# Feed-forward products of a four-layer decoder step in half blocks by seven products, with weight sums on POOL

## The reference

```
def causal_conv(x, buf, w):
    K = w.shape[0]
    T = x.shape[1]
    xp = jnp.concatenate([buf.astype(x.dtype), x], axis=1)
    y = xp[:, 0:T] * w[0]
    for j in range(1, K):
        y = y + xp[:, j:j + T] * w[j]
    return y, xp[:, T:]

def conv_ffn(x, buf, p, l):
    u, buf_new = causal_conv(x @ p['ffn_w_up'][l], buf, p['ffn_conv_w'][l])
    u = u + p['ffn_conv_b'][l]
    return (jax.nn.silu(u[..., :D_FF]) * u[..., D_FF:]) @ p['ffn_w_down'][l], buf_new
```

## Time and profile before

| | us |
|---|---|
| median of three runs | 3059.74 |
| lowest, highest | 3055.54, 3061.55 |
| the profiled execution | 3057.75 |
| its span, first to last instruction | 3056.1 |
| PE busy in it | 2891.5 (95%) |
| DVE busy | 1504.9 (49%) |
| ACT busy | 849.6 (28%) |
| POOL busy | 442.3 (14%) |

### The profile page before, as it was taken

One profiled execution on the slowest core, in us unless ns is written; L12 is line 12 of the kernel. 1 busy time (PEld: TensorE's weight loads), 2 busy tenths in 40 slices (PEclk: granted clock), 3 DMA queues, 4 the chain that ended last, 5 costly groups with the idle time before them and its releaser, 6 DMA issues.

```text
span 3056.1 us, 53572 instructions
## 1 busy us (share of the span) xinstructions
PE 2891.5 (95%) x20903; PEld 2108.9 (69%) x20903; DVE 1504.9 (49%) x2809; ACT 849.6 (28%) x2445; POOL 442.3 (14%) x1043
## 2 busy tenths in 40 slices
PE   7999999999988889999999899999998999989998
PEld 4788667766765567766766787867764678757765
DVE  7454548712333327741642454238715864438741
ACT  2334321102522221111555443211102134332111
POOL 0022111101222111101100221011100003202100
PEclk9999999999999999999999996799999999999999
DMA  5420123345223323333433013433342330123332
GB/s 160 146 57 7 44 91 121 115 119 120 67 77 92 89 74 111 124 114 112 138 101 101 6 40 95 131 124 120 109 121 87 118 98 5 30 76 110 124 105 83
DMA packets 401942, 287.48 MB, mean 94 GB/s; under 512 B 74956, under 2 KB 398077, under 8 KB 401309
## 3 DMA queue, kind: packets, MB, share of 16 engines
q1 hardware_dynamic: 382768, 267.03, 29.0%
q10 hardware_dynamic: 14828, 14.93, 1.5%
q0 software_dynamic: 4096, 2.11, 0.3%
HBM read 263.29 MB, written 20.73 MB: 93 GB/s over the span
## 4 chain that ended last, share of the span: by engine, by line
PE 88%; DVE 6%; ACT 2%; issue 2%; SPq 1%; DMA 1%; POOL 1%; ACTq 0%; DVEq 0%; POOLq 0%
PE bank L349 85%; SPq L2647 1%; PE bank L2821 1%; POOL arena L1345 1%; DMA arena<-cache_mla_latent 1%; PE bank L2844 0%; DVE h L1684 0%; DVE post_scaled L462 0%; DVE x L465 0%; PE bank L1297 0%; DVE small L1116 0%; DVE arena L1232 0%; DVE arena L1234 0%; DVE h L444 0%; DVE h L1683 0%
## 5 line engine op out<-in xcount | busy, mean ns | idle before, releaser
L349 PE MATMUL bank<-h,weights 128*128 128x320 f32 x3728 | 1018.4, 436 | 17.8 <-ACT h L431 17.8
L349 PEld LDWEIGHTS bank<-h,weights 128*128 128x128 f32 x3728 | 710.1, 191 | 322.3 <-issue 33.7
L349 PE MATMUL bank<-arena,weights 128*128 128x320 f32 (+4 forms) x3152 | 844.4, 434 | 15.5 <-DVE arena L1234 7.1
L349 PEld LDWEIGHTS bank<-arena,weights 128*128 128x128 f32 (+2 forms) x3152 | 584.1, 189 | 272.3 <-issue 26.2
L349 PE MATMUL bank<-arena 64*64 64x64 f32 (+8 forms) x2802 | 331.1, 289 | 9.7 <-DVE arena L2446 5.1
L462 DVE SCALAR_TENSOR_TENSOR post_scaled<-h,params,rstd 128x320 f32<-128x320 f32 x64 | 42.1, 658 | 543.9 <-ACT rstd L425 543.9
L349 PEld LDWEIGHTS bank<-arena 64*64 64x64 f32 (+3 forms) x2802 | 248.8, 163 | 35.7 <-issue 11.4
L1345 POOL TENSOR_TENSOR arena<-arena,consts 128x256 f32<-128x256 f32 x162 | 118.5, 736 | 779.9 <-DVE arena L1672 462.0
L570 ACT ACTIVATE arena<-bank 128x256 f32<-128x256 f32 x160 | 61.3, 383 | 541.0 <-PE bank L349 531.8
L638 DVE RECIPROCAL arena<-arena 128x336 f32<-128x336 f32 x88 | 197.6, 2246 | 0.0
L416 ACT ACTIVATE squares<-bank 128x320 f32<-128x320 f32 x64 | 28.0, 437 | 518.8 <-PE bank L349 518.8
(11 more groups left out here) (334 smaller groups left out, 3216.9 us busy)
## 6 DMA issues: line engine op xcount, KB each, us to landing
weights<-ffn_w_up SPq DMA_DIRECT2D x88, 1024.0 KB, 5.1
weights<-ffn_w_down SPq DMA_DIRECT2D x64, 704.0 KB, 4.7
weights<-rw_wrkv SPq DMA_DIRECT2D x24, 1024.0 KB, 5.3
weights<-gdn_w_in SPq DMA_DIRECT2D x24, 1024.0 KB, 5.4
arena<-cache_mla_latent SPq DMA_DIRECT2D x128, 128.0 KB, 2.3
weights<-rw_wo SPq DMA_DIRECT2D x8, 1024.0 KB, 5.4
weights<-gdn_wo SPq DMA_DIRECT2D x8, 1024.0 KB, 5.7
arena<-state_gdn_S SPq DMA_DIRECT2D x30, 256.0 KB, 4.0
```

What stands on the lines that cost most here:

```text
L349: return pe.matmul(out, lhsT, rhs, start=first, stop=last, skip_group_check=True)
```

## The change

Slots 3 to 21 of the up part, and all of the down part, are computed by seven products of half blocks (the Winograd form of Strassen's scheme): the weights of a slot are split in four quarters (two halves of the rows by two tiles of output), the activations in four (two halves of the k tiles by columns 0 to 159 and 160 to 319).

- PE makes m1, m6, m5, m7, m2, m3, m4 in this order, each over half of the k tiles, with 160 columns. Four banks serve a slot: m2 adds to m1, m4 to m7.
- POOL forms four sums of weight quarters for each slot (pool_sums) into one of three buffers; it gives its copies to ACT.
- DVE forms four sums of activation quarters (dve_mixes), once for H and in pieces for HFF after chunks 2, 3, 6, 7, 9 and 10, and combines the products out of PSUM.
- ACT takes over tap 2, the state columns, the kept rows, and the whole sigmoid as exp, ln(1 + e), exp.
- Down weights are loaded in 4 x 3 slots of 8, 8 and 6 k tiles by 256 columns. The turning of the last rows comes after the first pair of down tiles.

The diff, cut to its core:

```diff
+        def pool_sums(pool, key):
+
+            (a11, a12, a21, a22), (s1, s2, s3, s4) = quarters(key)
+            pool.wait_ge(*at(f"slot{where[key] % NS}", key))
+            if sum_of[key] >= NSUM:
+                pool.wait_ge(*at(*weight_used[summed[sum_of[key] - NSUM]]))
+            pool.tensor_tensor(s1, a21, a22, ALU.add).then_inc(*to("s1", key))
+            pool.wait_ge(*at("s1", key))
+            pool.tensor_tensor(s2, s1, a11, ALU.add).then_inc(*to("s2", key))
+            pool.tensor_tensor(s3, a11, a21, ALU.add).then_inc(*to("s3", key))
+            pool.wait_ge(*at("s2", key))
+            pool.tensor_tensor(s4, s2, a12, ALU.add).then_inc(*to("s4", key))
+
+        def dve_mixes(dve, dst, b1, b2, key):
+
+            b11, b12, b21, b22 = b1[:, :, 0:HN], b1[:, :, HN:NT], b2[:, :, 0:HN], b2[:, :, HN:NT]
+            t1, t2, t3, t4 = dst
+            dve.tensor_tensor(t1, b12, b11, ALU.subtract).then_inc(*to("mix1", key))
+            dve.tensor_tensor(t3, b12, b22, ALU.subtract).then_inc(*to("mix3", key))
...
+        def pe_fast_up(pe, l, c, half):
...
+            made = {"m1": ("fa", ("c11", key)), "m6": ("fb", ("c12", key)), "m5": ("fc", ("tt", key)), "m7": ("fd", ("c21", key))}
+            for step in PRODUCTS:
+                if step in made:
+                    ps = bank(pe, (made[step][0], key), made[step][1])[:, 0:HN]
+                elif step == "m2":
+                    ps = of(("fa", key))[:, 0:HN]
+                    pe.wait_ge(*at("s1c", key))
+                elif step == "m3":
+                    ps = of(("fb", key))[:, HN:NT]
+                    pe.wait_ge(*at("u2", key))
+                else:
+                    ps = of(("fd", key))[:, 0:HN]
+                    pe.wait_ge(*at("c22", key))
...
+                for k in range(4):
+                    ins = mm(pe, ps, a[:, k, :], b(k), k == 0 and step not in ("m2", "m4"), k == 3)
+                ins.then_inc(*to(step, key))
+            weight_used[key] = ("m4", key)
...
+            def gate_sigmoids(c):
+
+                for m in (2 * c, 2 * c + 1):
...
+                    act.activation(e, CONV[:, 0, m % 2, :], ACT.Exp, scale=-1.0).then_inc(*to("gate_e", (l, m)))
+                    act.wait_ge(*at("gate_e", (l, m)))
+                    act.activation(e, e, ACT.Ln, bias=1.0).then_inc(*to("gate_ln", (l, m)))
+                    act.wait_ge(*at("gate_ln", (l, m)))
+                    act.activation(e, e, ACT.Exp, scale=-1.0).then_inc(*to("gate_s", (l, m)))
...
+            for s in range(len(UP) + 1):
+                if s >= 1:
+                    first_taps(s - 1)
+                if FAST <= s < len(UP):
...
+                    act.activation(S1C[s % 2], of(("fa", key))[:, 0:HN], ACT.Copy).then_inc(*to("s1c", key))
+                if s >= 1:
+                    tails(s - 1)
...
+                if FAST <= s < len(UP):
...
+                    act.wait_ge(*at("m2", key))
+                    act.activation(XP[:, 2 * s % 4, 2:2 + HN], of(("fa", key))[:, 0:HN], ACT.Copy).then_inc(*to("c11", key))
+                if s >= 2 and s % 2 == 0:
+                    gate_sigmoids(s // 2 - 1)
+                if 1 <= s < len(UP) - 1:
+                    states(s + 1)
...
         def pool_ffn(pool, l):
             pool.wait_ge(*at("rstd", 4 * l + 2))
...
+            for s in range(FAST, len(UP)):
+                pool_sums(pool, slot_key(l, s))
+            for c in range(4):
+                for part in range(3):
+                    pool_sums(pool, ("down", l, c, part))
...
         def dve_ffn(dve, l):
             q = 4 * l + 2
             dve_scale_h(dve, q, ("up_done", (l, 1, 1)))
...
+            dve_mixes(dve, [UMIX[:, i] for i in range(4)], H[:, 0:4, :], H[:, 4:8, :], ("up", l))
...
+            for s in range(1, len(UP) + 1):
+                key = slot_key(l, s) if FAST <= s < len(UP) else None
+                conv(2 * s - 2)
+                if key:
...
+                    dve.tensor_tensor(U2, fb[:, 0:HN], S1C[s % 2], ALU.subtract).then_inc(*to("u2", key))
+                conv(2 * s - 1)
+                if key:
...
+                    dve.tensor_tensor(TT, fc[:, 0:HN], U2, ALU.add).then_inc(*to("tt", key))
+                    dve.wait_ge(*at("m7", key))
+                    dve.wait_ge(*at("tt", key))
+                    last_half(2 * s + 1, "c22", key, fd, TT, ALU.add)
+                if s % 2 == 0:
+                    gate(s - 2)
+                    gate(s - 1)
+                if key:
+                    dve.wait_ge(*at("m3", key))
+                    last_half(2 * s, "c12", key, fb[:, HN:NT], TT, ALU.subtract)
+                    dve.wait_ge(*at("m4", key))
+                    dve.tensor_tensor(XP[:, (2 * s + 1) % 4, 2:2 + HN], fd[:, 0:HN], U2, ALU.add).then_inc(*to("c21", key))
+                if s % 2 == 0 and s // 2 - 1 in MIXED:
```

More of the change, by code:

```diff
@@ L152 @@
     "rwkv_chunk_sums": "am inv y state m0 z sam m_new",
-    "ffn_taps": "tap1 tap2 conv",
-    "ffn_gate": "gate_d gate_gu gate_r hff",
+    "ffn_taps": "tap1 conv xp_zero",
+    "ffn_gate": "gate_gu hff",
+    "fast_products": "m1 m2 m3 m4 m5 m6 m7 part_done",
+    "fast_weights": "s1 s2 s3 s4",
+    "fast_activations": "mix1 mix2 mix3 mix4",
+    "fast_tiles": "u2 tt vv c11d c12 c21 c22",
+    "fast_copies": "s1c c11",
+    "ffn_sigmoid": "gate_e gate_ln gate_s",
+    "ffn_rows": "xp_state tail tap2",
     "residual": "x post",
@@ new lines, in build, with tile_pairs, quarters @@
+        UP = [(c, half) for c in range(11) for half in range(2)]
+        FAST = 3
+        summed = [key for l in range(layers) for key in
+                  [("up", l, half, c) for c, half in UP[FAST:]] + [("down", l, c, part) for c in range(4) for part in range(3)]]
+        sum_of = {key: i for i, key in enumerate(summed)}
+        def tile_pairs(key):
+            return DOWN_ROWS[key[3]][1] // 2 if key[0] == "down" else 4
+        def quarters(key):
+            kp = tile_pairs(key)
+            w = slot_view(where[key], 2 * kp, 256)
+            sums = arena(SUM0 + sum_of[key] % NSUM * 2048, 4, kp, P)
+            return [w[:, 0:kp, 0:P], w[:, kp:2 * kp, 0:P], w[:, 0:kp, P:256], w[:, kp:2 * kp, P:256]], [sums[:, i] for i in range(4)]
@@ L515, in build, with slot_key, xp_ready @@
         order = list(ffn_tiles())
-        def xp_step(l, n):
+        def slot_key(l, s):
+            return ("up", l, UP[s][1], UP[s][0])
+        def xp_ready(l, n):
             c, half, j, m = order[n]
-            return ("xp_first" if n < 4 else "xp", (l, half, m))
+            if n < 4:
+                return [("xp_first", (l, half, m))]
+            if n // 2 < FAST:
+                return [("xp", (l, half, m))]
+            return [("c22", slot_key(l, n // 2)), ("c21", slot_key(l, n // 2))] if j else \
+                   [("c11", slot_key(l, n // 2)), ("c12", slot_key(l, n // 2))]
         def pe_ffn(pe, l):
@@ L528, in pe_ffn @@
                 weight_used[("up", l, half, 0)] = ("up_done", (l, half, 1))
-            for n, (c, half, j, m) in enumerate(order):
+            for n, (c, half, j, m) in enumerate(order[0:2 * FAST]):
                 if n < 4:
@@ L540, in pe_ffn, with pe_tails @@
                 weight_used[key] = ("up_done", (l, half, m))
+            for c, half in UP[FAST:]:
+                pe_fast_up(pe, l, c, half)
+            for c in range(4):
+                pe_fast_down(pe, l, c)
+                if c == 0:
+                    pe_tails(pe, l)
+            pe_norm(pe, q + 1)
+        def pe_tails(pe, l):
             for g, (first, n) in enumerate([(0, 4), (4, 3)]):
@@ L576, in act_ffn @@
                     if m >= 2:
[L577 to L588, removed]
-                act.dma_start(rows[i * P:i * P + r, :], TOUT[0:r, 1 + i, :]).then_inc(*to("tail_stored", l, 16))
-            act_outputs(act, q + 1, ("tail_stored", l))
+                        act.wait_ge(*at("hff", (l, m - 2)))
@@ L635, in gate @@
[L635 to L641 removed]
+                dve.tensor_tensor(GD[:, 0, :], g, u, ALU.mult).then_inc(*to("gate_gu", (l, m)))
@@ L667, in build @@
+            dve_post_norm(dve, q + 1, lambda m: ("c21" if m % 2 else "c12", ("down", l, m // 2)))
         stage_x = arena(0, 3, D)
```

245 lines of the change are left out of this document (192 added, 53 removed).

## The result

The median went from 3057.64 us (3050.67 to 3061.55, four runs) to **3129.55 us** (3119.59 to 3132.02, four runs): a ratio of 1.0232, 95% interval 1.0202 to 1.0262. Slower, as forecast, and 25 us above the number given. The profiled execution took 3130.85 us, its span is 3129.1 us. The matmul helper of the changed kernel is L357. What follows is its last layer's feed-forward part, which runs from 2804 to 3109 us. From the pre-norm's last matmuls to the post-norm's first, each of the four layers took 276.8 us before and takes 294.9, 296.1, 296.8 and 295.6 us now: 76 us in all, where the whole span grew by 73. Each of the waits that the change brings to PE agrees within 0.5 us in the four layers.

What follows compares the result with a forecast made beforehand. PE's matmuls were taken to bound the kernel. Per layer, -33.2 (PE) + 34.9 (pairs) + 8 (start's wait) + 1.7 (half clock) = +11.4 us, times 4 = +46, giving 3105 us; range 2955 to 3180.

Steps and rivals of the forecast that it cites:

- PE's own part: Feed-forward matmuls: 1680 products of 160 columns at 135 ns replace 960 of 320, gaining 33.2 us a layer if PE never waits.
- PE's gain is no gain: Rival named with the experiments: the block scheme itself is no gain; no chance given.
- POOL's part: Weight sums: four additions of 512 columns a slot, 1.265 us each, 5.06 us a slot, fitting alone under 7.56.
- The lock: DVE and POOL exclude each other on SBUF operands; a sum ahead of a DVE operation costs 1.0 us, a handover saving 0.25.
- rival C: DVE and POOL handovers save nothing: 18 us a layer more, 3177 us; chance 0.02.
- A plain pair: Two up slots without mixing, scheduled by hand: 17.7 us instead of 15.1.
- one sum in its way: Step in the pair of slots: the second gate's last product meets one POOL sum and ends at 10.5 us.
- A mixing pair: Two up slots with DVE's mixing of gate tiles ahead: 20.0 us, against 16.9 without any lock.
- Rival B: PE's waits of 1 to 3 us in each pair bring half-clock windows, 15 us a layer, 3166 us; chance 0.08.
- The start: Up part's first slots: PE waits 8 us before m3 of slot 3, and half clock costs 1.7 us.
- The down part and end: Nothing waits in the down part; the last tile's extra DVE step adds 0.3 us a layer, within the rounding.
- Rival A: Sums fall into DVE's waits, pairs take 15.1 or 16.9 us, kernel faster at 2982 us; chance 0.33.

Runs made afterwards that it cites:

- x8: Changed kernel with taps' results in PSUM, block scheme from slot 6, and gate sigmoids ahead of the copy of c11: 3019.59 us, ratio 0.9891 to the kernel before.
- x4: Changed kernel with the scheme in the down part alone, up tiles direct and no mixes of h: 3014.51 us, ratio 0.9859 to the kernel before.
- x1: Changed kernel with every POOL sum replaced by a fill of the same tile, all waits kept: 2959.46 us, ratio 0.9682 to the kernel before.
- x5: Changed kernel with the taps' middle results in free columns of the slot's PSUM banks, from slot 3 on: 3116.61 us, ratio 1.0214 to the kernel before.
- x2: Changed kernel with ScalarE's gate sigmoids ahead of the copy of c11: 3121.9 us, ratio 1.0219 to the kernel before.
- x11: Changed kernel with taps' results in PSUM and gate sigmoids ahead of the copy of c11, scheme from slot 3: 3046.87 us, ratio 0.9978 to the kernel before.

## Why the prediction was right, and where its size was off

Slower, inside the range and near the number. Forecast were +11.4 us a layer; measured +19.0 on average, +18.8 in the last one, whose miss of 7.4 is taken apart here.

- **PE's own part: right.** 136 ns for 160 columns (135 forecast; of 1680 x 0.9 ns = 1.5 us a layer, 0.9 are in the pairs below and 0.5 in the down part), 84.4 us for the down part with its transposes (83 forecast without them, 0.8 more with). A slot without waits takes 7.6 us in x8. Rival "PE's gain is no gain" falls with x4.
- **POOL's part: right.** 1.27 us a sum alone (1.265), and no sum is a releaser of PE.
- **The lock: right, and it is the cause.** x1 shows that without reads on POOL the loss is gone, x5 that a tap passes at its own length beside whole sums, and x8 that the sums cost a plain pair nothing once the chain doesn't lie beside them. A handover saved more than the 0.25 us taken: two taps in a row start 1.54 and 1.37 us apart, where a tap and a sum alone are 0.57 + 1.27 = 1.84, so 0.3 to 0.5. That refutes rival C: by the Trainium skill (SBUF — State Buffer, Who interferes with whom) each instruction blocks the other until it has finished, and nothing would be saved. The trace agrees with the exclusion and not with its full length.
- **A plain pair: 18.1, forecast 17.7.** The hand schedule had c22 of the even slot at 7.1; the trace has 2933.41 - 2926.27 = 7.1. It had the second gate's last product end at 10.5; it ends at 2937.74 - 2926.27 = 11.5. The step that failed is "one sum in its way": both pieces of that product, 256 and 64 columns, met a sum (1.33 and 1.29 us). The odd slot gave most of this 1.0 us back: 1.4 us of sums were put in its way, and one tap met one (1.65 us), so its c22 came at 16.9, forecast 16.6. 4 x 0.4 = 1.6 us a layer.
- **A mixing pair: 20.9, forecast 20.0.** The mix makes u2 late, PE waits 2.06 us at once, and half clock follows: 2.30 us from m4's start to the next m1 instead of 1.09. Rival B, given 0.08, is true in these pairs and wrong in the plain ones, whose gaps of 0.4 to 0.5 us left the clock at 1.00. With the last pair as it came, the nine took 3024.63 - 2848.28 = 176.3 us where 170.8 were forecast: 5.5 of the 7.4 us missed.
- **The start: size right, in part by luck, since the place was wrong.** 7.65 us of waiting (8), 1.7 of half clock (2843.28 to 2847.19 for 16 instructions, 3.91 instead of 2.17). But PE waited before m2 for ScalarE's copy s1c, not before m3 for u2. The step that failed is ScalarE's part, where only the order of sigmoids and c11 was weighed: at the start, s1c of slot 3 stands in ScalarE's program behind the copies of slot 2, six sigmoid operations and two taps, and these behind DVE's convolutions, held by the sums. ACT's timeline:

```profile
2838.77 0.49 ACT L749 ACTIVATE arena<-arena 128x336 f32<-128x336 f32 x1
...
2841.84 1.21 ACT L730 ACTIVATE arena<-arena,params 128x336 f32<-128x336 f32 x2
2842.95 0.28 ACT L766 ACTIVATE small<-bank 128x160 f32<-128x160 f32 x1
```

- **The down part and end: "nothing waits", wrong at the end.** The last tile's extra step was put at 0.3 us and left out of the sum; PE waits 1.36 us for POOL's squares there, and 1.5 us pass that didn't before. Within the down part PE doesn't wait. A wait of 1.40 us just ahead of it, for u2 of the last up slot, wasn't forecast either and is in the ninth pair above; half clock followed it, though rival B was argued down with a gap of 1.3 us that left the clock at 1.00.
- **Rival A** (the sums fall into DVE's waits) was wrong by its own point: the pairs average 19.6 us, above its 17.7. It is what x8 makes true, by moving what DVE does instead of the sums.
- **PE's idle time** in the up part is 11.6 + 11.4 + 7.0 = 30 us in the last layer, where some 40 were forecast and under 25 would have spoken for A. The rest of what the up part lost isn't idle time in the records: half clock, and a fraction of a us at each of 35 waits.
- Together: 5.5 (pairs) + 0.5 (down part) + 1.5 (end) - 0.1 (start) = 7.4 us, the whole miss of the last layer. Open stays why the layers differ by up to 1.9 us at nearly equal waits.

## What to carry to other kernels

A helper engine's busy share (POOL 31% here) says little when it and the engine that feeds the bottleneck hold each other up, as DVE's taps of 0.57 us took 1.34 to 1.65 beside POOL's sums: take the operations of both that have all their operands in SBUF, lay them out over one period by hand, and see which of them stand in the chain to the next period. Where such a chain has two causes in series (here collisions and a late sigmoid), removing one only uncovers the other, so test the edits together as well as alone: in the four layers of the profiles x2 gave 1 us and x5 10, neither told by the intervals of the medians, and both together (x11) gave 80. A scheme that pays in one stage and not in another can be used in that stage alone (x4).

## What the hardware showed beside that

- Whether DVE passes beside POOL went by one operand: 567 ns on 336 columns when a tap read one input from PSUM (x5), 1.0 to 1.1 us on average when all lay in SBUF, at the same place of the program.
- A fill on POOL (0.53 us for 512 columns) left DVE's taps at 563 ns (x1).
- Idle gaps of 2.06 to 2.08 us on PE, and one of 1.40, were followed by half clock within the next 16 instructions in all five mixing pairs of the last layer; gaps of 0.4 to 0.5 us never. In the last layer of x8 one of four gaps of 2.13 us was followed by none, nor was one of 1.51, so the gap's length alone doesn't decide.
